# Moving the tiles of a three-pass dense kernel to other places in on-chip memory

## The reference, cut to what matters

```
h = h + 0.5 * swiglu(rmsnorm(h), w1, w3, w2)          # w1, w3: 1024 x 2816, w2: 2816 x 1024
z = rmsnorm(h) @ w_in                                 # attention and state-space mixer behind it
h = h + concat(o_nsa, o_s5) @ w_out
h = h + 0.5 * swiglu(rmsnorm(h), ...)                 # the same again
h = h + sigmoid(rmsnorm(h) @ w_ple_gate) * (p @ w_ple)
for l in range(2):                                    # second block
    u = (rms_norm(x) * (1 + scale) + shift) @ w_in_2[l]     # 1024 x 5120
    y = concat(y_rg, y_ml) @ w_out_2[l]                     # 2048 x 1024
    x = x + gate * y
out = rms_norm(x)
```

## Time and profile before

| | |
|---|---|
| median of 3 runs | 2183.66 us (2183.04 to 2184.3) |
| the profiled execution's own time | 2186.03 us |
| its span, first to last instruction | 2184.3 us |
| TensorE's matmuls busy | 2049.7 us, 94% of the span |
| VectorE busy | 1278.4 us, 59% |
| ScalarE busy | 817.3 us, 37% |
| GpSimd busy | 356.7 us, 16% |
| mean granted TensorE clock | 0.96 of full speed |

### The profile page before, as it was taken

How to read it: one execution, slowest core, us unless ns; L and a number is a source line. 1 busy time by engine, 2 the same in 40 slices (tenths; PEclk the granted TensorE clock), 3 DMA queues, 4 the chain that set the end, 5 groups by cost and what they waited for, 6 DMA issues and landing times.

```text
span 2184.3 us, 22175 instructions
## 1 busy us (share of the span) xinstructions
PE 2049.7 (94%) x8726; PEld 1539.1 (70%) x8726; DVE 1278.4 (59%) x1837; ACT 817.3 (37%) x1207; POOL 356.7 (16%) x319
## 2 busy tenths in 40 slices
PE   7999999988888899999999899899999898999997
PEld 5888888755544488888887677676778676856785
DVE  6763344669797445655555676724773558435842
ACT  5331333201233543312333348343542455434531
POOL 2000001165333010000011202301201014102002
PEclk9999999998788999999999899899999899999998
DMA  4232332221000135645642132221122222220221
GB/s 177 97 112 81 97 103 90 83 78 44 11 1 1 63 135 174 201 166 164 199 138 68 49 103 78 77 84 42 49 96 90 84 85 68 68 87 29 83 92 58
DMA packets 53175, 196.72 MB, mean 90 GB/s; under 512 B 5968, under 2 KB 6480, under 8 KB 52432
## 3 DMA queue, kind: packets, MB, share of 16 engines
q1 hardware_dynamic: 42912, 159.50, 22.3%
q0 software_dynamic: 7504, 28.58, 4.1%
q10 hardware_dynamic: 2656, 7.23, 1.0%
HBM read 192.14 MB, written 2.10 MB: 89 GB/s over the span
## 4 chain that ended last, share of the span: by engine, by line
PE 81%; DVE 10%; ACT 3%; POOL 3%; DMA 1%; issue 1%; SPq 0%; POOLq 0%; DVEq 0%; ACTq 0%
PE PS L531 81%; DVE AR L1705 2%; POOL AR L2134 1%; DVE HX L1813 1%; DVE AR L1801 1%; DVE WLO L1474 1%; DVE HNL L1477 1%; ACT WHI L1021 1%; DVE TMP L1477 1%; DMA RAW<-in_w_in 0%; DMA RAW<-in_w13a 0%; DVE ACC L1477 0%; ACT HX L1184 0%; PE PS L726 0%; DVE AR L1690 0%
## 5 line engine op out<-in xcount | busy, mean ns | idle before, releaser
L531 PE MATMUL PS<-HNH,WHI 128*128 128x512 f32 x1632 | 670.2, 411 | 18.4 <-ACT HNH L1052 13.7
L1474 DVE TENSOR_TENSOR WLO<-RAW,WHI 128x1024 fp32r<-128x1024 f32 (+1 forms) x270 | 368.8, 1368 | 526.7 <-ACT WHI L1021 526.7
L531 PE MATMUL PS<-HNH,WLO 128*128 128x512 f32 x1632 | 652.4, 400 | 21.7 <-DVE WLO L1474 21.7
L1021 ACT ACTIVATE WHI<-RAW 128x1024 fp32r<-128x1024 f32 (+1 forms) x270 | 296.2, 1097 | 754.6 <-PE PS L531 669.8
L531 PE MATMUL PS<-HNL,WHI 128*128 128x512 f32 x1632 | 448.3, 397 | 0.2
L531 PEld LDWEIGHTS PS<-HNH,WHI 128*128 128x128 f32 x1632 | 310.0, 190 | 109.9 <-issue 23.0
L531 PEld LDWEIGHTS PS<-HNH,WLO 128*128 128x128 f32 x1632 | 310.8, 190 | 105.1 <-DVE WLO L1474 22.8
L531 PEld LDWEIGHTS PS<-HNL,WHI 128*128 128x128 f32 x1632 | 307.5, 188 | 76.7 <-DVE HNL L1477 2.0
L531 PE MATMUL PS<-AR 128*128 128x512 f32 (+12 forms) x700 | 214.4, 519 | 13.7 <-DVE SQ L1694 4.5
L2052 POOL TENSOR_TENSOR ACC<-ACC,SQ 128x512 f32<-128x512 f32 x46 | 62.8, 1364 | 796.5 <-ACT SQ L1036 795.5
L531 PEld LDWEIGHTS PS<-AR 128*128 128x128 f32 (+5 forms) x700 | 98.7, 194 | 96.5 <-issue 59.2
(11 more groups left out here) (293 smaller groups left out, 2482.5 us busy)
## 6 DMA issues: line engine op xcount, KB each, us to landing
RAW<-in_w_in SPq DMA_DIRECT2D x80, 512.0 KB, 3.5
AR<-in_w_ada POOLq DMA_DIRECT2D x48, 512.0 KB, 3.8
RAW<-in_w13a SPq DMA_DIRECT2D x44, 512.0 KB, 3.3
RAW<-in_w13b SPq DMA_DIRECT2D x44, 512.0 KB, 3.6
RAW<-in_w_out SPq DMA_DIRECT2D x40, 512.0 KB, 3.6
RAW<-in_w2a SPq DMA_DIRECT2D x16, 704.0 KB, 4.1
RAW<-in_w2b SPq DMA_DIRECT2D x16, 704.0 KB, 5.0
RAW<-in_w_inA SPq DMA_DIRECT2D x12, 512.0 KB, 3.3
```

What stands on the lines that cost most here:

```text
L531: return pe.matmul(o, l, r, start=start, stop=stop, skip_group_check=True)
L1021: act.activation(hi_of(name, i), raw_of(name, i), ACT.Copy).then_inc(*HI.up(name, i))
L1474: dve.tensor_tensor(lo_of(name, i), raw_of(name, i), f32(hi_of(name, i)), S_).then_inc(*LO.up(name, i))
```

## The change

Only places move. Every instruction, its shape, its order on its engine and the semaphores it waits for are the same as before, row by row on all five engines. In bytes from the start of the tile H, which does not move (in brackets the remainder by 256):

| tile | before | after |
|---|---|---|
| WHI | 178,400 (224) | 16,384 (0) |
| WLO | 195,296 (224) | 33,280 (0) |
| TMPH | 49,152 (0) | 50,176 (0) |
| RAW | 161,504 (224) | 79,328 (224) |
| AR, OH, YRH | 78,304 (224) | 96,224 (224) |
| YRL | 111,200 (96) | 129,120 (96) |
| HIDH | 106,976 (224) | 134,112 (224) |
| HIDL | 129,504 (224) | 156,640 (224) |
| OL | 139,744 (224) | 157,664 (224) |
| HNH | 16,384 (0) | 179,424 (224) |
| HNL | 32,768 (0) | 195,808 (224) |

A slot of WHI or WLO is 5,632 bytes, a piece of weight in it 512 bytes, a tile of the stream 2,048 bytes. Pieces and tiles therefore keep the remainder of their first by 256. The constants, the small vectors and RS move up by 1,024 bytes.

```diff
         H = tiles_(sb("H", KD * T))
-        at_hn = at[0]
-        HNH, HNL = tiles_(sb("HNH", KD * T, F32R)), tiles_(sb("HNL", KD * T, F32R))
-        HX = place("HX", at_hn, 2 * KD * T)
+        NSLOT, SLOT, NW = 3, 1408, 3
+        WHI, WLO = sb("WHI", NW * SLOT, F32R), sb("WLO", NW * 1408, F32R)
         at_tmp = at[0]
...
         LA = sb("LA", 6 * 16)
+        RAW = sb("RAW", NSLOT * SLOT)
         NAR = 20800
         at_ar = at[0]
         AR = sb("AR", NAR)
-        NSLOT, SLOT = 3, 1408
-        RAW = sb("RAW", NSLOT * SLOT)
-        NW = 3
-        WHI, WLO = sb("WHI", NW * SLOT, F32R), sb("WLO", NW * SLOT, F32R)
+        at_hn = at[0]
+        HNH, HNL = tiles_(sb("HNH", KD * T, F32R)), tiles_(sb("HNL", KD * T, F32R))
+        HX = place("HX", at_hn, 2 * KD * T)
         assert base + 4 * at[0] <= 229344, at[0]
-        HIDH, HIDL = tiles_(place("HIDH", at_ar + 7168, 11 * T, F32R)), tiles_(place("HIDL", at_ar + 7168 + 11 * T, 11 * T, F32R))
+        HIDH, HIDL = tiles_(place("HIDH", at_ar + 9472, 11 * T, F32R)), tiles_(place("HIDL", at_ar + 9472 + 11 * T, 11 * T, F32R))
...
-        SMALL = AR[:, 20512:20512 + 256]
+        SMALL = AR[:, 9216:9216 + 256]
         RHO = AR[:, 20784:20800]
-        STMP = ar(18432, 2048)
+        STMP = ar(7168, 2048)
```

## The result

The changed kernel takes 2194.3 us (median of five runs, 2192.4 to 2196.2) against 2183.7 us: a ratio of 1.005, with a 95% interval of 1.0034 to 1.0066. It is slower by 10.6 us, or 0.5%, where 29.3 us of gain was forecast. The profiled execution has 2193.9 us, its span 2192.1; against the profile of before the span is longer by 7.8 us.

The account below looks back on a forecast made before the run. TensorE was taken to bound the kernel, its matmuls busy for 94% of the span and 81% of the chain on PE. Only HNH and HNL counted: 2183.7 - 29.3 = 2154.4 us, range 2144 to 2196.

Parts of the forecast that it names:

- Height: Reading that low-lying moved tiles (HNH, HNL) are slow and high ones fast; the prediction set it aside because of YRL.
- Step 1: HNH and HNL, 4,896 matmuls: going from remainder 32 to 224 makes them fast, 4,400 x 6.67 ns = 29.3 us gained.
- Step 2: HIDH, HIDL, OH, OL, 1,248 matmuls going from remainder 0 to 224: no change, at most 8.3 us lost.
- Step 3: w_out_2: YRL stays slow from 128 to 96; TMPH from 32 to 0 gains at most 0.9 us, taken as 0.
- Step 4: Attention, scan and memory fp32 matmuls, and 96 of 280 columns loading HNH: 0.6 us either way, nothing in the sum.
- Step 5: VectorE, ScalarE, GpSimd and DMAs working on other places: durations unchanged, taken as 0.
- Only an exact match is fast: Rival, chance 0.22: remainder 0 alone is good, HNH and HNL gain nothing, matching tiles lose; 2193.1 us.
- No effect: Rival, chance 0.12: levels belong to the stages, not to places; 2183.7 us.
- the mixed case: Rival, chance 0.08: only the normed stream HNH and HNL gains, the others lose; 2162.7 us.
- The rule of the Trainium skill: Says PE has separate read ports for moving operand and weight load and never waits; by it the sum would be zero.
- A level below 0.2267 us: Rival, chance 0.07: a step below the fast level, 0.2200 us a matmul, 67 us gained; 2116.7 us.

Follow-up runs that it names:

- pad8_after: The changed kernel with eight unused words (32 bytes) ahead of RAW, so every moved tile but YRL matches the weights by 256 bytes; 2155.2 us.
- pad8_before: The kernel before with eight unused words ahead of AR, so HNH and HNL also match the weights by 256 bytes; 2154.8 us.
- weights_plus96: The kernel before with only the weight halves WHI and WLO moved up by 96 bytes; 2193.9 us.
- weights_plus224: The kernel before with only the weight halves WHI and WLO moved up by 224 bytes; 2172.4 us.
- slots_skewed: pad8_before with the second and third weight slots starting 4 and 16 bytes late, and WLO 32 bytes later in every slot; 2187.6 us.
- low_half_off: pad8_before with eight more unused words between WHI and WLO, so WHI matches and WLO stands 32 bytes off; 2188.0 us.

## Why the prediction was wrong

**What bounds the kernel, and the property that decides** were right. The chain stayed at 81% on PE, and the remainder by 256 between moved tile and weights, read from YRL against HIDL, gave the right level for every tile at 0, 32 and 128 in the kernels that followed, wherever both halves of the weights stood alike. Height was ruled out by pad8_after and pad8_before. That two reads get in each other's way was the prediction's assumption; the runs show how the pitch depends on the two starts, and what happens inside stays open.

**Step 1 failed**: it took the fast level for HNH and HNL at 224, a value that no row showed, on the strength of one sentence: "If there is one connected slow range, it holds 32 and 128 and not 0; then 224 is fast unless the range comes round to it." It comes round. weights_plus96 and weights_plus224 show 160, 192 and 32 slow, the changed kernel 224, and slots_skewed shows 252 slow, one word from a match. Of the values measured only 0 itself is fully fast, and 4 bytes beside it are slow. Of the three values in the trace of before, one was fast and two were slow, which was reason to ask how wide "fast" is before taking a new value as fast. Step 1's gain of 29.3 us came to nothing: HNH and HNL changed by 0.2 us in all.

**Its size was right for another edit**, in part by luck. A real match gives nearly the same as 4,400 x 6.67 ns: 28.9 us by the median (2183.7 to 2154.8), 28.8 us in the pitches of HNH and HNL. But these are 4,741 dense pitches and 6.1 ns each, HNL 6.6 and HNH 5.8, so a count too low and a price too high cancelled.

**Step 2** rested on the same reading and put this term at nothing, and the loss came: 8.3 us stated as the upper end, 8.1 us measured in HIDH, HIDL, OH and OL. **Step 3** was right that YRL stays slow, but TMPH and YRH moved, by -0.4 and +1.0 us. **Step 4** is too small to read: the median pitches of the matmuls of 280 columns are 0.128 to 0.130 us before and 0.128 to 0.131 after. **Step 5** held, by the groups of 1000 to 1100 us in the changed kernel, which answer to the earlier trace rows:

```profile
L1473 DVE TENSOR_TENSOR WLO<-RAW,WHI 128x1024 fp32r<-128x1024 f32 x17 | 20.8, 1223 | 26.0 <-ACT WHI L1020 26.0
L1020 ACT ACTIVATE WHI<-RAW 128x1024 fp32r<-128x1024 f32 x18 | 19.1, 1063 | 46.5 <-PE PS L530 46.5
L1649 DVE TENSOR_TENSOR HIDL<-TMP,HIDH 128x512 fp32r<-128x512 f32 x9 | 6.2, 692 | 6.3 <-ACT HIDH L1107 6.3
```

All within 1 ns.

**The rivals.** *Only an exact match is fast* named the property, its place and its price, 2193.1 us against 2194.3 measured, and the point from which it decides, that 224 behaves like 32. It is also the reason why the measured time lies inside the range of 2144 to 2196, whose upper end was set by it and not by the forecast. Given that two of three known values were slow, its chance of 0.22 was small against 0.45. *No effect* and the mixed case are out. The rule of the Trainium skill from which the prediction drew that no place matters ("SBUF — State Buffer", section "Who interferes with whom") does not hold for these matmuls at full clock: 39 us lie between two kernels that differ by 32 bytes of padding. A level below 0.2267 us was seen nowhere at full clock. (The floor of 0.2125 that step 1 takes from half clock is 0.2133 when it is read from the means, 0.4267 / 2; nothing hangs on it.)

## What to carry to other kernels

Where float32r matmuls stand close together at full clock, compare the pitches of groups that differ only in the tile they move; a difference of 3% is worth an unused 32 bytes. Lay out moved tiles and weight slots so that their starts, and the steps between slots and pieces, differ by multiples of 256 bytes. Work this out for every operand after each change of layout, since any tile whose size is no multiple of 256 bytes shifts all behind it; in slots_skewed eight words more for WHI shifted WLO as well. Only 512-column matmuls with 128-column loads in float32r were measured. And when a rule is read from few values, a new value needs to be known to lie inside the good range, and these rows did not show how wide that is.

## What the runs showed of the hardware that was not expected

- A float32r matmul of 512 columns behind a 128-column load has 0.2267 us at the least here and 0.2333 to 0.2343 at most other places, by the remainder of the two starts by 256 bytes; a step of one word loses the fast level (slots_skewed).
- The value 64 gives 0.2291 us, so there are more than two levels.
- Fast to slow and slow to fast are not instant. In the kernel before, the first seven pitches of HIDH behind HNL, from 145.18 us on the earlier trace rows, have 0.232 us on average, and only from the eighth on are they at 0.227.
- If one of two alternating weight pieces does not match, the whole stretch is slow (0.2340 us in low_half_off). Half a match is worth little: 2188.0 us, against 2154.8 with a full one and 2193.9 with none (weights_plus96).
- At half clock none of this exists. A tile at 32 has 0.4267 us on average in the kernel before (0.425 by the two decimals of the earlier trace rows), and HNH in pad8_before, where it matches, has 1.71 / 4 = 0.4275 at a granted clock of 0.50, which is 512 columns at 1.2 GHz:

```profile
1821.57 0.63 PE L532 MATMUL PS<-HNH,WHI 128*128 128x512 f32 x1
...
1823.28 0.63 PE L532 MATMUL PS<-HNH,WHI 128*128 128x512 f32 x1
```
